# The attention's values product as three fp32r passes, with the probabilities split on ScalarE and on GpSimd or VectorE

## What is computed

```python
def attend(blk):
    qn, qr = blk
    s = jnp.einsum("bqhd,bkhd->bhqk", qn, k_nope) + jnp.einsum("bqhr,bkr->bhqk", qr, k_rope)
    p = jax.nn.softmax(s.astype(F32) * scale, axis=-1).astype(v.dtype)
    return jnp.einsum("bhqk,bkhd->bqhd", p, v)
```

## Time and profile before

| | |
|---|---|
| median of three runs | 1700.0 us (1694.19 to 1701.23) |
| the profiled execution's own time | 1701.48 us |
| its span in the trace | 1699.4 us |
| attention in the trace, first exponential of unit 0 to last output copy | about 685 to 923 us |
| one head of eight units, heads 1 to 6 | 30.6 us |
| PE busy over the span | 1571.0 us, 92% |
| DVE, ACT, POOL busy over the span | 1050.5, 722.7, 351.1 us |

### The profile page before, as it was taken

How to read it: one execution, slowest core, us unless ns; L and a number is a source line. 1 busy time by engine, 2 the same in 40 slices (tenths; PEclk the granted TensorE clock), 3 DMA queues, 4 the chain that set the end, 5 groups by cost and what they waited for, 6 DMA issues and landing times.

```text
span 1699.4 us, 15517 instructions
## 1 busy us (share of the span) xinstructions
PE 1571.0 (92%) x5758; PEld 1047.3 (62%) x5758; DVE 1050.5 (62%) x1024; ACT 722.7 (43%) x720; POOL 351.1 (21%) x190
## 2 busy tenths in 40 slices
PE   5999989999989999999998997099999999999997
PEld 2444458764334444555555886078888888888774
DVE  6311243551532346467766564869999998999886
ACT  5201100021432211434443143067777777777773
POOL 0400000000000000314446341403322342224304
PEclk9999989999999999999999998589999999999999
DMA  5605100052100000000012235869999999999995
GB/s 187 223 0 217 36 0 1 0 93 73 44 6 0 0 0 0 25 1 21 5 37 88 81 118 177 306 236 367 379 369 379 378 379 368 379 379 378 379 370 212
DMA packets 152852, 284.40 MB, mean 167 GB/s; under 512 B 25268, under 2 KB 35842, under 8 KB 152803
## 3 DMA queue, kind: packets, MB, share of 16 engines
q1 hardware_dynamic: 147187, 263.28, 43.7%
q0 software_dynamic: 4464, 16.25, 3.6%
q10 hardware_dynamic: 1152, 4.19, 0.6%
HBM read 259.07 MB, written 24.64 MB: 167 GB/s over the span
## 4 chain that ended last, share of the span: by engine, by line
PE 83%; DVE 7%; ACT 4%; DMA 4%; issue 2%; POOL 0%; POOLq 0%; ACTq 0%; SPq 0%; DVEq 0%
PE psum L1042 16%; PE psum L1391 9%; PE psum L1393 9%; PE psum L1392 9%; PE psum L1269 6%; PE psum L1205 4%; PE psum L1077 3%; PE psum L1026 3%; DMA arena<-in_exp_w_down 3%; PE psum L1175 2%; PE psum L1315 2%; PE psum L1317 2%; PE psum L1316 2%; PE psum L1088 2%; PE psum L1087 2%
## 5 line engine op out<-in xcount | busy, mean ns | idle before, releaser
L1815 DVE TENSOR_TENSOR split_at<-arena,split_at 128x2048 fp32r<-128x2048 f32 x188 | 427.6, 2290 | 61.8 <-ACT split_at L921 60.0
L921 ACT ACTIVATE split_at<-arena 128x2048 fp32r<-128x2048 f32 x192 | 367.5, 1916 | 64.2 <-PE psum L1393 54.1
L1391 PE MATMUL psum<-split_at,split_at 128*128 128x512 f32 x768 | 306.4, 399 | 1.4 <-DVE split_at L1821 1.4
L1393 PE MATMUL psum<-split_at,split_at 128*128 128x512 f32 x768 | 300.6, 391 | 0.0
L1392 PE MATMUL psum<-split_at,split_at 128*128 128x512 f32 x768 | 299.9, 391 | 0.0
L1042 PE MATMUL psum<-arena 128*128 128x512 f32 (+1 forms) x608 | 267.0, 598 | 3.7 <-DVE arena L1502 3.7
L1042 PEld LDWEIGHTS psum<-arena 128*128 128x128 f32 (+1 forms) x608 | 113.9, 188 | 152.4 <-issue 147.8
L1393 PEld LDWEIGHTS psum<-split_at,split_at 128*128 128x128 f32 x768 | 144.8, 189 | 31.4
L1391 PEld LDWEIGHTS psum<-split_at,split_at 128*128 128x128 f32 x768 | 145.0, 189 | 29.8 <-DVE split_at L1821 1.8
L1392 PEld LDWEIGHTS psum<-split_at,split_at 128*128 128x128 f32 x768 | 145.2, 189 | 28.4
L1269 PE MATMUL psum<-arena 128*128 128x512 f32 x256 | 120.8, 594 | 6.2 <-ACT arena L830 5.4
(11 more groups left out here) (282 smaller groups left out, 2235.8 us busy)
## 6 DMA issues: line engine op xcount, KB each, us to landing
arena<-in_exp_w_gate SPq DMA_DIRECT2D x64, 1024.0 KB, 14.2
arena<-in_exp_w_up SPq DMA_DIRECT2D x64, 1024.0 KB, 14.1
arena<-in_exp_w_down SPq DMA_DIRECT2D x64, 1024.0 KB, 14.2
arena<-in_w_in SPq DMA_DIRECT2D x9, 1024.0 KB, 5.4
arena<-in_x SPq DMA_DIRECT2D x8, 512.0 KB, 4.1
xhat_scratch<-arena SPq DMA_DIRECT2D x8, 512.0 KB, 6.1
arena<-in_w_out SPq DMA_DIRECT2D x8, 512.0 KB, 3.6
arena<-xhat_scratch SPq DMA_DIRECT2D x8, 512.0 KB, 4.9
```

Of the source, the lines that this page charges most:

```text
L921: a(flat(wsplit[c % WS][0]), wraw[:, c], ACT.Copy).then_inc(s_whi, 1)
L1391: mm(bank(out_bank), src[0][:, k, :], whi[:, k % 4, :], start=(k == 0), stop=False)
L1393: ins = mm(bank(out_bank), src[1][:, k, :], whi[:, k % 4, :], start=False, stop=(k == KT - 1))
L1815: tt(flat(lo), wraw[:, c], flat(hi), ALU.subtract).then_inc(s_wlo, 1)
```

## The change

The values and the probabilities are split like queries and keys. `v_copy` now makes a rounded copy of the values, `v_hi` (a cast), and the rest `v_lo` (a subtraction), both on GpSimd. ScalarE writes the exponential to one of three buffers `p32`, and a second ScalarE instruction, `probs_high`, copies it rounded to one of two buffers `p_hi`. The rest, `p_lo = p32 - p_hi`, is written over `p32` by GpSimd for units kb = 2 to 6 of heads 0 to 6, and by VectorE for kb = 0, 1 and 7, for all of head 7, and for kb = 4 of head 6. `pv(n)` becomes two fp32r products for each half (v_hi x p_hi, v_lo x p_hi), and `pv_low(n)` a third (v_hi x p_lo), which stands one unit later. A high part's buffer is free again when the rest's product of two units before is done; an exponential's buffer, three units before.

The order lists move: of the eight weight blocks one each goes to kb = 1 of heads 3, 4, 5, two to head 6 (kb = 1 and 5) and three to head 7 (kb = 1, 3, 5); the other mixers' rests go to the end of heads 1 and 2. Some semaphores elsewhere are merged, with their counts changed and the same waits. The core of the diff:

```diff
+        v_hi, v_hi32 = rounded("values_high", 43984, 2, KT, 2 * DV)
+        v_lo, _ = rounded("values_low", 32720, 2, KT, DV)
+        p_hi, p_hi32 = rounded("probs_high", 25552, 2, T)
+        p32 = [mem(at, T) for at in (46032, 47056, 27600)]
...
+        WOUT_AT = [TT * h + qt for h, qt in ((3, 1), (4, 1), (5, 1), (6, 1), (6, 5), (7, 1), (7, 3), (7, 5))]
...
+        GROUPS_AT = [TT * h + qt for h, qt in ((1, 4), (1, 5), (2, 4), (2, 5))]
...
+        LOW_DVE = [n for n in range(N_UNIT) if n % TT in (0, 1, 7) or n // TT == NH - 1 or n == TT * (NH - 2) + 4]
+        LOW_POOL = [n for n in range(N_UNIT) if n not in LOW_DVE]
...
-                    pool.wait_ge(s_pv, TT * (h - 1))
-                pool.tensor_copy(v1[:, h % 2, :, 0:DV], v_at[:, :, DV * h:DV * h + DV]).then_inc(s_vs, 1)
+                    pool.wait_ge(s_pvl, TT * (h - 1))
+                values = v_at[:, :, DV * h:DV * h + DV]
+                link(pool.tensor_copy(v_hi[:, h % 2, :, 0:DV], values))
+                pool.tensor_tensor(v_lo[:, h % 2], values, v_hi32[:, h % 2, :, 0:DV], ALU.subtract).then_inc(s_vs, 1)
...
+                pool.wait_ge(s_ph, n + 1)
+                pool.tensor_tensor(p_lo[n % 3], p32[n % 3], p_hi32[:, n % 2, :], ALU.subtract).then_inc(s_plp, 1)
...
             def probs(n):
                 act.wait_ge(s_qk, n + 1)
+                if n >= 3:
+                    act.wait_ge(s_pvl, n - 2)
+                a(p32[n % 3], bank(2 * (n % 2), 2), ACT.Exp).then_inc(s_exp, 1)
+
+            def probs_high(n):
+                act.wait_ge(s_exp, n + 1)
                 if n >= 2:
-                    act.wait_ge(s_pv, n - 1)
-                a(p_at[:, n % 2, :], bank(2 * (n % 2), 2), ACT.Exp).then_inc(s_exp, 1)
+                    act.wait_ge(s_pvl, n - 1)
+                a(p_hi[:, n % 2, :], p32[n % 3], ACT.Copy).then_inc(s_ph, 1)
...
             def o_copy(h):
-                act.wait_ge(s_pv, TT * (h + 1))
+                act.wait_ge(s_pvl, TT * (h + 1))
...
                 h, qt = divmod(n, TT)
+                probs_high(n)
                 if h and qt == 0:
                     o_copy(h - 1)
...
                 for j in range(2):
-                    ins = mm(bank(6 + j), v1[:, h % 2, kb, :], p_at[:, n % 2, HALF * j:HALF * j + HALF], start=(kb == 0), stop=(kb == TT - 1))
-                ins.then_inc(s_pv, 1)
+                    p = p_hi[:, n % 2, HALF * j:HALF * j + HALF]
+                    mm(bank(6 + j), v_hi[:, h % 2, kb, :], p, start=(kb == 0), stop=False)
+                    mm(bank(6 + j, 1, 0, DV), v_lo[:, h % 2, kb, :], p, start=False, stop=False)
+
+            def pv_low(n):
...
+                for j in range(2):
+                    ins = mm(bank(6 + j), v_hi[:, h % 2, kb, :], p_lo[n % 3][:, HALF * j:HALF * j + HALF], start=False, stop=(kb == TT - 1))
+                ins.then_inc(s_pvl, 1)
...
+                if n and kb == 0:
+                    pv_low(n - 1)
                 if n + 1 < N_UNIT:
                     scores(n + 1)
...
+                if kb:
+                    pv_low(n - 1)
                 pv(n)
...
+                if n in LOW_DVE and not (h == NH - 2 and kb == 4):
+                    probs_low(n)
                 if h + 1 < NH and kb in MAX_FIRST:
                     row_max(h + 1, MAX_FIRST[kb], 4)
```

More of the change, by code:

```diff
@@ L542, in _ @@
             pool.wait_ge(s_hp, len(HEADS))
-            link(pool.memset(v1, 1.0))
+            link(pool.tensor_copy(v_hi.rearrange("p a k d -> p (a k) d")[:, :, DV:], ones[:, 0:DV].unsqueeze(1).to_broadcast([P, 2 * KT, DV])))
             v_copy(0)
@@ L1285, in _ @@
                     rough_next(h + 1, MAX_SECOND[kb])
+            pv_low(N_UNIT - 1)
             def x1_turn(i):
@@ L1729, in _ @@
                     row_max(h + 1, MAX_SECOND[kb], 4)
+                if h == NH - 2 and kb == 4:
+                    probs_low(n)
                 if h + 1 < NH and kb == ROWS_AT:
```

57 lines of the change are left out of this document (35 added, 22 removed).

## The result

The changed kernel takes **1739.3 us** (median of 4 runs, 1735.2 to 1741.1) against 1699.5 for the kernel before on the same chip: a ratio of 1.0239, 95% interval 1.0216 to 1.0262. The prediction said 1747, range 1707 to 1765, and slower at 0.83.

The account below looks back on a forecast made before the run. TensorE's own time was taken to set attention, except waits at head ends and for row maxima. Heads 1 to 6's starts 34.2, head 6 5.5, head 7 6.6, head 0 0.3 sum to +46.6: forecast 1747 us, range 1707 to 1765.

Parts of the forecast that it names:

- TensorE's saving: Values' products in attention: 1.72 to 1.39 us, 0.33 a unit, 0.14 with rough products; 21 us over 64 if nothing else moved.
- ScalarE's copy: One rounded copy a unit, about 1.0 us, hidden except at a head's end, where unit 8's stands in front of `o_copy`.
- The walk: Step-by-step timing of a head's end from the next head's first scores (0): 34.95 us a head against 30.58, +4.4.
- VectorE's rests and multiplies are blocked by GpSimd's: Head starts: two-SBUF-input VectorE operations and GpSimd's exclude each other; a blocked 128x1024 one ends about 1.1 us after GpSimd's.
- Who goes next: Where two VectorE operations stand in line, GpSimd's waiting one gets in between, and VectorE's second waits for it.
- The weight blocks in heads 3 to 5: Block ahead of unit 10 on GpSimd: unit 9's rest ends at 16.1, rough product starts at 20.0; +5.3 us in place of +4.4.
- Head 6: Second weight block ahead of unit 53's rest on GpSimd: rest until 11.8, wanted at 6.9; +5.5 us with VectorE's extra subtraction.
- Head 7: Last head: GpSimd has only weight blocks, VectorE every rest, blocked by them; `o_copy` until 34.5 against 27.9, +6.6 us.
- no exclusion: Rival: these subtractions don't block each other, VectorE's chain alone counts; 1694 us, chance 0.07.
- The fp32 pace: Rival: the values' passes run at 0.43, no TensorE gain and the waits on top; about 1765 us, chance 0.03.
- Half as often: Rival: same exclusion with fewer collisions, VectorE first at 12.2, 2.3 us a head off; about 1728 us, chance 0.2.
- The full saving: Rival: VectorE's and GpSimd's work spread so nothing waits; 1679 us, or 1685 with the maxima's 4.1; chance 0.06.

Follow-up runs that it names:

- e1: Changed kernel with six fp32r passes alone: exponential written rounded, no second ScalarE copy, no probabilities' rests; 1685.9 us, ratio 0.9919.
- e2: Changed kernel with ScalarE's rounded copy but no probabilities' rests made; pv_low multiplies by p_hi again; 1701.2 us, ratio 1.0004.
- e5: Changed kernel with GpSimd's subtractions and weight-block scalings in attention replaced by equally long writes that read nothing; values' cast stays; 1725.8 us, ratio 1.0159.
- e9: Changed kernel with GpSimd only writing, and the weight blocks' scaling and rest replaced by one write of 0.95 us; 1702.2 us, ratio 1.0012.
- e3: Changed kernel without VectorE's 31 rests of the probabilities; pv_low reads p_hi for those units; GpSimd keeps all its work; 1723.0 us, ratio 1.0142.
- e8: Changed kernel without GpSimd's scaling and rest of the eight weight blocks, a memset in their place; 1723.6 us, ratio 1.0126.
- e10: e2 with one edit: o_copy ahead of probs_high at a head's first unit; 1700.9 us, ratio 1.001.

## Why the prediction was right, step by step

- **TensorE's saving.** Right. Predicted 0.33 us a unit, 0.14 with rough products, which is 4 x 0.33 + 4 x 0.14 = 1.9 a head; e1's heads are 1.7 shorter.
- **ScalarE's copy.** Mis-sized. The walk let it cost at a head's end alone, as the copy in front of `o_copy`. It costs 15 us by itself (e2 less e1), 3.2 of them in head 0, and some 6 of the 15 by the clock (four stretches of 3.4 us, at most 1.6 each; the one in head 0 is among the 3.2). Head 0, predicted at 0.3 over before, is 1.6 over (29.3 for 27.7).
- **VectorE's rests and multiplies are blocked by GpSimd's.** Right, and shown by e5; over-sized in the walk. Head 1 was predicted at 34.95 and took 35.1, but by two errors that cancel. From the 0 (scores of unit 8 at 710.90) the rough product that waits for the maximum should start at 19.1 and starts at 16.5 (727.38). The failed step is "the rest of unit 9 on VectorE is behind it and ends at 15.6": that rest started at 720.53 and took its own 1.21, while GpSimd's cast waited. One reason is that head 0 has no head before it to divide, so VectorE has none of the reciprocals and multiplies in head 1's first units that the walk puts ahead of the rests of units 7 and 8. What is left of the head was to take 15.85 and took 18.6, since TensorE's clock fell right there (2.5 of the 2.75, above). Head 2 comes out alike: 21.2 predicted, about 18.7 measured (764.67), with a fall behind it.
- **Who goes next.** The walk lets GpSimd in between two of VectorE's operations in line, as at the earlier trace rows. That held in four places of heads 1 to 6 (VectorE's rests at 755.63, 785.70, 791.55 and 860.96 take 3.3), and in four others VectorE's multiply and rest both went ahead of a GpSimd subtraction that waited for the two:

```profile
751.18 0.73 DVE L1771 TENSOR_TENSOR arena<-arena 64x256 f32<-64x256 f32 x1
751.60 3.72 POOL L558 TENSOR_TENSOR split_at<-arena,split_at 96x1024 fp32r<-96x1024 f32 x1
751.84 1.21 DVE L1763 TENSOR_TENSOR probs_low<-arena,probs_high 128x1024 fp32r<-128x1024 f32 x1
```

  (The others are the rests at 748.16, 825.50 and 894.92.) No run shows what decides. And the rest of kb = 1 ran ahead of GpSimd's of kb = 2 in all six heads, which is the other order that the prediction gave as a sign of a wrong size.
- **The weight blocks in heads 3 to 5.** The walk put nearly all of the 5.3 down to exclusion, the block adding 0.9. Measured: 5.2, 4.7 and 3.5 over before, and the 4.7 of head 4 have up to 2.5 of the clock's in them. But e5 has 4.8, 3.7 and 3.6 over it without any exclusion, and e9, which is e5 without blocks, is 0.1 to 0.7 under before in these heads. This is the step whose reason was wrong while its sum roughly held: unit 10's rest, last in GpSimd's line, is as late by itself as the chain through VectorE. Head 3 was over-sized (38.0, measured 35.8).
- **Head 6.** Right in what delays it, and in its number with the clock's help: 41.4 predicted, 41.6 measured, of which the low clock from 925.0 to 931.6 has up to 2.4; 41.9 in e5 and in e3. As the walk had it, a block and a rest stand in line there, with no exclusion in it; e8, without blocks, has 32.4.
- **The clock.** Not in the prediction at all: every term took passes at 0.23. It falls at the new waits and costs at most 12.4 us, and so it hides most of what the walk had too high. That is luck.
- **Head 7.** Over-sized: +6.6 predicted, +2.4 measured. The failed step is "the first block takes 9.5 to 12.3 and 12.6 to 14.9, around a blocked multiply; the rest of 10, ready at 10.4, ends at 16.0": it took GpSimd's scaling of a block, one input in SBUF, to hold VectorE up for a whole instruction.

The last point was left open between 1747 and 1740, and the trace of after settles it. Timeline, two places in head 7, then one in head 3 (L580 is the scaling, L1771 VectorE's multiply, L1763 its rest):

```profile
939.86 2.85 POOL L580 TENSOR_SCALAR arena<-arena 128x1024 f32<-128x1024 f32 x1 [10.91 <-ACT split_at L893]
...
940.49 0.76 DVE L1771 TENSOR_TENSOR arena<-arena 64x256 f32<-64x256 f32 x1
941.18 1.21 DVE L1763 TENSOR_TENSOR probs_low<-arena,probs_high 128x1024 fp32r<-128x1024 f32 x1
...
951.91 2.84 POOL L580 TENSOR_SCALAR arena<-arena 128x1024 f32<-128x1024 f32 x1
...
952.12 1.98 DVE L1763 TENSOR_TENSOR probs_low<-arena,probs_high 128x1024 fp32r<-128x1024 f32 x1 [2.46 <-ACT probs_high L848]
...
796.68 4.24 POOL L580 TENSOR_SCALAR arena<-arena 128x1024 f32<-128x1024 f32 x1
...
797.07 1.21 DVE L1763 TENSOR_TENSOR probs_low<-arena,probs_high 128x1024 fp32r<-128x1024 f32 x1
```

A rest that starts in the middle of the scaling takes its own 1.21; one that starts 0.21 behind its start is held up 0.77, to 954.10, while the scaling runs to 954.75. The multiply at 940.49, 0.63 behind the scaling's start, is held up by 0.34. In each case VectorE is free again 1.0 us behind the scaling's start (940.83 and 952.89), and none waits for its end. The other way round, the scaling that met VectorE's multiply and rest at 796.7 took 1.4 longer. The Trainium skill, "SBUF — State Buffer", section "Who interferes with whom", has a VectorE instruction with two SBUF inputs contend with a GpSimd instruction that reads SBUF for a lock that is exclusive, and the order of issue decides who blocks. For GpSimd's two-input operations these traces agree that the block is a whole one (723.54 and 723.55, above), though the rest at 751.84 ran ahead of a subtraction that had issued at 751.60; for the one-input scaling the block lasts for 1.0 of its 2.84 us.

The rivals: "no exclusion" was priced at 1694 with the blocks in place, and e5, which is that case, took 1725.8, since that rival gave a rest that is late in GpSimd's queue no price. The fp32 pace is ruled out by e1. "Half as often", at 1728, is 11 us off, but its mechanism is nearer to the trace than the forecast's: exclusion with the order of kb = 1 and 2 the other way, GpSimd in between in four places of eight. 1739.3 less the clock's 12 is 1727. The full saving showed only where nobody made copies or rests. 1739.3 is 7.7 under the forecast: heads 1 to 6 are 4.0 less, head 7 4.2 less and head 0 1.3 more, 6.9 in the trace. The verdict, the place and the kind of the waits were right; without the clock the forecast would have been up to 20 us too high, so the nearness of the number is luck for a good part.

What stays open: the clock's fall was not tried by itself. Its cost is read from e2's heads and from the pace in the stretches, and what brings it on is not settled. Nor is why the last head takes 28.1 us in e9 and 25.6 in e5, which has the weight blocks besides.

## What to carry to other kernels

Before work is given to an engine for its idle time, see what it will stand beside and behind: GpSimd was busy for a fifth of the span here, but for 88 of attention's 236 us, and two-input operations on it and on VectorE shut each other out, and its queue alone made the rests late. Two causes that delay the same event don't add, so removing one can show little; take them away singly and together before calling either small. Read the granted clock beside each such run: waits that are taken away can take a low clock with them, and then the difference is worth more than the wait. And a chain that leaves TensorE for 4 us says nothing of how long TensorE stands still: read its own idle time beside the chain before pricing what a shorter list would save.

## What the runs showed of the hardware

- GpSimd and VectorE: an operation of VectorE with two inputs in SBUF that starts behind one of GpSimd with two inputs waits out the whole of it (2.63 for a multiply of 0.42; e5's mean is 1220 ns for the rests where GpSimd only writes, 1624 where it reads). When a multiply and a rest of VectorE stand in line, GpSimd's waiting subtraction gets in between in some places (755.63) and waits for both in others (751.60). With GpSimd's one-input scaling VectorE is held up only for the first 1.0 of its 2.84 us, by 0.8 at the most (952.12), and the scaling by what VectorE has in line (1.4 at 796.68).
- TensorE's granted clock falls behind some waits and not behind others of the same length. In e2 the product of a head's first unit waits 1.69 or 1.70 us in every head, and the windows around it in heads 1 and 2 are

```profile
719.00:724.00 5.00, 4.17 (x18) 3.25 (x19) 4.19 (x4) 4.21 (x5) 4.73 (x4) 1.00 0.01 3
749.00:754.00 5.00, 4.34 (x12) 3.26 (x13) 4.79 (x5) 2.66 (x4) 4.71 (x4) 0.66 0.01 3
```

  and so on in turn, 1.00 in heads 3 and 5, 0.66 in heads 4 and 6. In e10 it is heads 3, 4 and 6. What decides between them no run here shows.
- A weight pass of 64 columns costs what one of 128 does, 0.23 us with 512 moving columns.
